# A two-block transformer layer stack on one core: the opening is reordered, TensorE makes three of the eight modulation products, GpSimd none, and VectorE builds the rotation tables after the first activations

## The chip, the cores and the metric

The kernel runs on one core of one Trainium2 chip. The core has five engines with instruction queues of their own: TensorE (PE in the rows), VectorE (DVE), ScalarE (ACT), GpSimd (POOL) and SyncE (SP), which here only issues DMAs. They meet at semaphores alone. The metric is the device time of one execution in microseconds; before the change three timed runs took 1609.88, 1611.33 and 1612.16 us, median 1611.33.

## The reference, cut to what matters

All arithmetic is float32. One sequence of 256 tokens with width 1024 passes a first block (modulated norm, recurrent branch, dilated attention) and a second one (two layers of feed-forward, mixing and embedding parts). The change touches only how the first block begins:

```python
inv_freq = ROPE_THETA ** (-jnp.arange(0, ROT_DIM, 2) / ROT_DIM)
ang = positions[..., None] * inv_freq
cos, sin = jnp.cos(ang), jnp.sin(ang)
c_act = jax.nn.silu(c)                        # c: [1, 1024]
mod = c_act @ w_mod[l] + b_mod[l]             # w_mod: [1024, 3072]
shift, scale, gate = jnp.split(mod, 3, axis=-1)
h = rms_norm(x, g_norm[l]) * (1.0 + scale) + shift
proj = h @ w_in[l]                            # w_in: [1024, 8192]
x_rnn, z_rnn, q, k, v, z_attn, g_r, g_a = jnp.split(proj, IN_SPLITS, axis=-1)
...
qh = apply_partial_rope(q, cos, sin)
kh = apply_partial_rope(k, cos, sin)
```

`shift` and `scale` must be known before the first activation `h`, and `h` before any product with `w_in`. The tables `cos` and `sin` are needed first when q is rotated.

## The kernel before, in words

All weights come from HBM as 245 units of 1 MB (128 partitions by 2048 floats), in the order of use, through a ring of four buffers `raw` (`RING = 4`). Units 0 to 7 hold the shift and scale columns of `w_mod`, 128 rows of it each ("modulation units" 0 to 7 below); the next units are weights proper, called w0, w1, w2, w3 (together the projection to q) and so on. SyncE issues every transfer in one fixed order, and each waits until the buffer's previous content has been used.

A weight unit is split into two parts before TensorE uses it: ScalarE rounds it (`whi`, line 367, `hi`), and the remainder `wlo = raw - whi` is made by VectorE for three units of four (line 1047, `lo`) and by GpSimd for the fourth (line 920). TensorE then makes three products for each piece (lines 1741 to 1743): 12 matmuls of 128x512 for one unit and one half of the tokens. The work of block one goes in slots: 8 slots are a group of four units, first for tokens 0 to 127 (t = 0), then for tokens 128 to 255 (t = 1). The order on each engine is written out by hand; nothing reorders it.

The opening before the change:

- VectorE zeroes `mod_part`, then makes the angles and reduces them to the range of the sine in a chain of small instructions (lines 1149 to 1186), then normalizes the two halves of the rows (line 1189, `xn`).
- The modulation is a product of one row with a 1024x2048 matrix. Unit r times the r-th column of `c_act` gives a 128x2048 product. VectorE adds up six of them (lines 1197 and 1202, `mod_part`), GpSimd makes those of units 0 and 3 (line 959, `MOD_POOL = (0, 3)`, `mod_pool`). TensorE sums each of the three tiles over its partitions: 16 matmuls with one column of ones (line 1864, into `aux`). VectorE adds the three sums and the bias (lines 1207 to 1213, `mod`, `scale_g`).
- TensorE transposes the normalized rows (line 1794, `turn`), VectorE applies scale and shift (line 1221, `full`), ScalarE rounds (line 441, `feed_hi`), VectorE makes the remainder (line 1233, `feed_lo`). With two signals `first_fed` for t = 0 and two for t = 1 TensorE may start the products.
- VectorE then makes a few small vectors of the recurrent gate (lines 1239 to 1268) and waits for the sums of q. ScalarE copies them (line 448), VectorE rotates (lines 1137 to 1142, `rotate`), and TensorE transposes the rotated half at the last slot of the group (slot 7, `block1_turns`), ahead of the last unit of t = 1.

ScalarE applies the sine to the two tables early (lines 431 and 432), before it rounds the first weight unit.

Of the kernel before, what the change touches and what calls it, by code (L numbers as in the profile page):

```python
# [91 lines left out]
MOD_POOL = (0, 3)  # L92
# [10 lines left out]
def build(nc, io):  # L103
    with ExitStack() as ctx:
# [8 lines left out]
        def sb(name, shape, dtype=F32):  # L113
# [69 lines left out]
        mod_pool = [placed("mod_pool0", [P, 2 * D], F32, base[0]),  # L183
                    placed("mod_pool1", [P, 2 * D], F32, base[0] - 4 * HEADS * SEQ)]
# [80 lines left out]
        setup_loaded = sem("setup_loaded")  # L265
        x_loaded = sem("x_loaded")
# [11 lines left out]
        mod_pooled = sem("mod_pooled")  # L278
        mods_ready = sem("mods_ready")
        mod_summed = sem("mod_summed")  # L280
# [53 lines left out]
        def mod_count(r):  # L334

            return sum((k in MOD_POOL) == (r in MOD_POOL) for k in range(r + 1))

        def wait_mod(engine, r):
            engine.wait_ge(mod_pooled if r in MOD_POOL else mod_used, mod_count(r))

# [12 lines left out]
        def _(act):  # L353
# [67 lines left out]
            act.wait_ge(setup_loaded, 16 * 3)  # L421
# [4 lines left out]
            act.wait_ge(lam_abs, 1)  # L426
            act.activation(tiny[:, 2, :], tiny[:, 1, :], ACT.Exp, scale=-1.0).then_inc(lam_exp, 1)
            act.wait_ge(lam_abs, 2)
            act.activation(lb[:, :], tiny[:, 9, 0:A_HEADS], ACT.Sigmoid).then_inc(lb_ready, 1)
            act.wait_ge(angles_ready, 1)  # L430
            act.activation(sin_t[:, :, :], sin_t[:, :, :], ACT.Sin).then_inc(tables_ready, 1)
            act.activation(cos_t[:, :, :], cos_t[:, :, :], ACT.Sin).then_inc(tables_ready, 1)
            hi(RING - 1)

            for t in range(TOK):
                if t:
                    hi()
                for i in range(2):
                    b = next_turn()
                    act.wait_ge(moved[b], (n["tb"] - 1) // 2 + 1)  # L440
                    act.activation(feed_hi[:, 4 * i:4 * i + 4, lanes(t)], full[:, 4 * i:4 * i + 4, lanes(t)],
                                   ACT.Copy).then_inc(fed_hi, 1)

# [445 lines left out]
        def _(pool):  # L889
# [66 lines left out]
            pool.wait_ge(c_ready, 1)  # L956
# [67 lines left out]
        def _(dve):  # L1024
# [120 lines left out]
            mark(dve.memset(mod_part[:, :], 0.0))  # L1145
            dve.wait_ge(setup_loaded, 16 * 3)
# [8 lines left out]

            mark(dve.tensor_copy(pos_f[:, :], pos_i[:, :]))
# [30 lines left out]
            for t in range(TOK):  # L1187
                r = next_rstd()
                dve.tensor_scalar(xn[:, t, :], h[:, t, :], r, None, ALU.mult).then_inc(staged_dve, 1)  # L1189

            dve.wait_ge(c_ready, 1)
            for r in range(N_MOD1):
                if r in MOD_POOL:
                    continue
                dve.wait_ge(loaded[r % RING], 16 * (r // RING + 1))
                if r < N_MOD1 - 1:
                    dve.scalar_tensor_tensor(mod_part[:, :], raw[:, r % RING, :], c_act[:, r:r + 1], mod_part[:, :],
                                             ALU.mult, ALU.add).then_inc(mod_used, 1)
                    dve.wait_ge(mod_used, mod_count(r))
                else:  # L1200
                    for part, signal in ((slice(0, D), mods_ready), (slice(D, 2 * D), mod_used)):
                        dve.scalar_tensor_tensor(mod_part[:, part], raw[:, r % RING, part], c_act[:, r:r + 1],
                                                 mod_part[:, part], ALU.mult, ALU.add).then_inc(signal, 1)
            lo(2)

            dve.wait_ge(mod_summed, 1)
            mark(dve.tensor_tensor(mod[:, :], aux[:, 0, 0:2 * KC], cols[:, COL["b_mod"]:COL["b_mod"] + 2 * KC], ALU.add))
            settle()
            for i in range(len(MOD_POOL)):
                at = 2 * KC * (i + 1)  # L1210
                mark(dve.tensor_tensor(mod[:, :], aux[:, 0, at:at + 2 * KC], mod[:, :], ALU.add))
                settle()
            mark(dve.scalar_tensor_tensor(scale_g[:, :], mod[:, KC:2 * KC], 1.0,
                                          cols[:, COL["g_norm"]:COL["g_norm"] + KC], ALU.add, ALU.mult))
            settle()
# [1043 lines left out]
```

## Time and profile before

| | us |
|---|---|
| median of three timed runs | 1611.33 |
| span of the profiled execution | 1609.2 |
| TensorE busy in the span | 1477.0 |
| first product with a weight unit begins | 52.88 |
| transposes of the first rotated half begin | 73.14 |

The profiled execution is known by its span, from the first to the last instruction; its own device time is not listed apart, so 1609.2 us stands for it. The median of the timed runs is 2.1 us above. Times in rows are from the start of the span. A timeline row merges neighbours of one kind: start, time from the first start to the last end, engine, line, tiles, count, and in brackets how long the engine had been idle and what ended that. One matmul with f32 operands appears as two records in the rows of `aux` and `turn`.

### The profile page before, as it was taken

Reading aid. Unit: us, or ns where it says so; the run is one execution under the profiler, and the core shown is the slowest. Engines: PE = TensorE matmul, PEld = TensorE weight load, DVE = VectorE, ACT = ScalarE, POOL = GpSimd, SP = SyncE. Lnnn points to the kernel's source line nnn. Section 1 sums busy time; section 2 is a strip of 40 time slices with the busy share of each in tenths; the row PEclk is TensorE's granted clock in tenths of the full one; section 3 lists DMA queues with packets and bytes.
Section 4 is the critical chain, followed back from the end, with each engine's and each line's share of the span. In section 5 each row is a group of like instructions: output and inputs, shape, how many; then the busy total and the mean of one; then the engine's idle time right before and its main releaser. Section 6 shows DMA issues by size and latency. Waiting matters only on the chain.

```text
span 1609.2 us, 17128 instructions
## 1 busy us (share of the span) xinstructions
PE 1477.0 (92%) x6606; PEld 1212.3 (75%) x6606; DVE 852.5 (53%) x757; ACT 706.2 (44%) x692; POOL 377.8 (23%) x153
## 2 busy tenths in 40 slices
PE   3999889898999988889999989999999979999896
PEld 3788677676888877667887867878888848888785
DVE  8734775866334457446434474452673343654344
ACT  2545747334344436134444344443443443444332
POOL 3122212213122222003112131222322332322112
PEclk9999999999999999579999999999999979999998
DMA  6745234645455453106544455554643522654441
GB/s 270 292 157 210 105 105 156 236 157 201 162 200 185 163 224 142 46 1 216 184 163 167 179 204 188 209 192 147 234 177 141 206 105 105 229 184 163 169 163 40
DMA packets 40508, 272.51 MB, mean 169 GB/s; under 512 B 4865, under 2 KB 5889, under 8 KB 8834
## 3 DMA queue, kind: packets, MB, share of 16 engines
q1 hardware_dynamic: 36992, 261.65, 44.5%
q10 hardware_dynamic: 3458, 10.04, 1.8%
q8 instruction: 43, 0.70, 0.2%
q14 instruction: 15, 0.12, 0.0%
HBM read 270.62 MB, written 1.05 MB: 169 GB/s over the span
## 4 chain that ended last, share of the span: by engine, by line
PE 73%; DVE 15%; ACT 5%; POOL 3%; issue 3%; DMA 2%; DVEq 0%; SPq 0%; ACTq 0%; POOLq 0%
PE acc L1741 22%; PE acc L1743 22%; PE acc L1742 22%; DVE wlo L1047 5%; PE turn L1794 3%; ACT whi L367 2%; POOL wlo L920 2%; DMA raw<-in_units 1%; DVE h L1117 1%; DVE xn L1101 1%; DVE gate_part L1435 1%; DVE feed_lo L1085 1%; DVE red L1178 0%; DMA gpost<-in_norm_g 0%; PE turn L1895 0%
## 5 line engine op out<-in xcount | busy, mean ns | idle before, releaser
L1047 DVE TENSOR_TENSOR wlo<-raw,whi 128x2048 fp32r<-128x2048 f32 x175 | 463.6, 2664 | 346.5 <-ACT whi L367 346.5
L1741 PE MATMUL acc<-whi,feed_hi 128*128 128x512 f32 (+1 forms) x1504 | 605.8, 403 | 38.9 <-DVE wlo L1047 15.9
L1743 PE MATMUL acc<-whi,feed_lo 128*128 128x512 f32 (+1 forms) x1504 | 593.3, 394 | 0.0
L1742 PE MATMUL acc<-wlo,feed_hi 128*128 128x512 f32 (+1 forms) x1504 | 593.2, 394 | 0.0
L367 ACT ACTIVATE whi<-raw 128x2048 fp32r<-128x2048 f32 x233 | 445.3, 1916 | 326.6 <-PE acc L1743 298.2
L1741 PEld LDWEIGHTS acc<-whi,feed_hi 128*128 128x128 f32 x1504 | 288.6, 192 | 103.2 <-DVE wlo L1047 16.2
L1743 PEld LDWEIGHTS acc<-whi,feed_lo 128*128 128x128 f32 x1504 | 288.0, 191 | 61.9
L1742 PEld LDWEIGHTS acc<-wlo,feed_hi 128*128 128x128 f32 x1504 | 288.9, 192 | 57.3 <-issue 0.2
L928 POOL TENSOR_TENSOR wlo<-raw,whi 128x2048 fp32r<-128x2048 f32 x29 | 133.9, 4618 | 519.9 <-ACT whi L367 519.9
L920 POOL TENSOR_TENSOR wlo<-raw,whi 128x2048 fp32r<-128x2048 f32 x29 | 141.1, 4867 | 393.1 <-ACT whi L367 393.1
L1741 PE MATMUL acc<-whi,hid_hi 128*128 128x512 f32 x352 | 137.8, 392 | 0.0
L1743 PE MATMUL acc<-whi,hid_lo 128*128 128x512 f32 x352 | 137.1, 389 | 0.0
L1742 PE MATMUL acc<-wlo,hid_hi 128*128 128x512 f32 x352 | 137.0, 389 | 0.0
L1464 DVE TENSOR_TENSOR hid_lo<-turn,hid_hi 128x512 f32 (+2 forms) x48 | 30.8, 641 | 88.4 <-ACT hid_hi L595 88.4
L1741 PEld LDWEIGHTS acc<-whi,hid_hi 128*128 128x128 f32 x352 | 66.2, 188 | 13.5
L1743 PEld LDWEIGHTS acc<-whi,hid_lo 128*128 128x128 f32 x352 | 66.1, 188 | 13.7
L1742 PEld LDWEIGHTS acc<-wlo,hid_hi 128*128 128x128 f32 x352 | 66.1, 188 | 13.5
L1794 PE MATMUL turn<-ident,xn 128*128 128x128 f32 x250 | 37.6, 293 | 36.8 <-DVE xn L1189 20.3
L595 ACT ACTIVATE hid_hi<-turn 128x512 f32 (+2 forms) x48 | 26.3, 548 | 99.2 <-PE turn L1794 99.2
L1794 PEld LDWEIGHTS turn<-ident,xn 128*128 128x128 f32 x250 | 31.2, 151 | 43.8 <-issue 23.7
L1455 DVE SCALAR_TENSOR_TENSOR hid<-acc,pre_rs,sgl 128x512 f32<-128x512 f32 (+1 forms) x48 | 33.7, 703 | 48.9 <-ACT sgl L588 43.4
L409 ACT ACTIVATE feed_hi<-turn 128x512 fp32r<-128x512 f32 x52 | 28.9, 592 | 69.8 <-PE turn L1794 69.7
(302 smaller groups left out, 1011.4 us busy)
## 6 DMA issues: line engine op xcount, KB each, us to landing
raw<-in_units SPq DMA_DIRECT2D x245, 1024.0 KB, 4.9
gpost<-in_norm_g ACTq DMA_DIRECT2D x8, 512.0 KB, 4.4
gpre<-in_norm_g ACTq DMA_DIRECT2D x6, 512.0 KB, 6.4
h<-in_x SPq DMA_DIRECT2D x1, 1024.0 KB, 5.9
w_ax<-in_w_ax SPq DMA_DIRECT2D x1, 1024.0 KB, 9.2
bgate<-in_b_gate SPq DMA_DIRECT2D x1, 1024.0 KB, 11.4
out<-h SPq DMA_DIRECT2D x2, 512.0 KB, 2.6
decay<-in_decay ACTq DMA_DIRECT2D x1, 768.0 KB, 4.1
```

The lines of the kernel that those rows point to most:

```text
L367: act.activation(whi[:, u % RING, :], raw[:, u % RING, :], ACT.Copy).then_inc(hi_ready, 1)
L409: act.activation(dst[:, 4 * i:4 * i + 4, lanes(t)], turn[:, b, :].rearrange("p (c s) -> p c s", c=4), ACT.Copy).then_inc(fed_hi, 1)
L595: act.activation(dst, turn[:, b, 0:P * count].rearrange("p (c s) -> p c s", c=count), ACT.Copy).then_inc(fed_hi, 1)
L920: pool.tensor_tensor(wlo[:, RING - 1, :], raw[:, RING - 1, :], whi[:, RING - 1, :].bitcast(F32), ALU.subtract).then_inc(pool_lo, 1)
L928: pool.tensor_tensor(wlo[:, RING - 1, :], raw[:, RING - 1, :], whi[:, RING - 1, :].bitcast(F32), ALU.subtract).then_inc(pool_lo, 1)
L1047: dve.tensor_tensor(wlo[:, u % RING, :], raw[:, u % RING, :], whi[:, u % RING, :].bitcast(F32), ALU.subtract).then_inc(lo_ready, 1)
L1455: dve.scalar_tensor_tensor(hid[:, t, 0:tiles, :], up, pre_rs[:, t:t + 1], sgl[:, t, 0:tiles, :], ALU.mult, ALU.mult)\
L1464: dve.tensor_tensor(hid_lo[:, at, lanes(t)], turn[:, b, 0:P * count].rearrange("p (c s) -> p c s", c=count), hid_hi[:, at, lanes(t)].bitca ...
L1741: pe.matmul(out, xh, wh, start=first, stop=False)
L1742: pe.matmul(out, xh, wl, start=False, stop=False)
L1743: return pe.matmul(out, xl, wh, start=False, stop=last)
L1794: last = pe.transpose(turn[:, b, P * i:P * i + P], part, ident[:, :])
```

## The change

`MOD_POOL = (0, 3)` becomes `MOD_PE = (1, 3, 7)`. TensorE takes units 1, 3 and 7 straight from `raw`: 16 matmuls each, with the unit's 128x128 pieces as weights and the unit's column of `c_act` as the one moving column. VectorE multiplies unit 0 (which also replaces the zeroing) and adds units 2, 4, 5 and 6; TensorE sums that one tile with the ones. GpSimd has no product. Four sums of 16 columns are added in one reduction. `pos_cols` and `invf` are issued by ScalarE. SyncE issues w0 ahead of modulation unit 7. VectorE makes one `lo` before the scales and two (not one) after t = 0. The angles and tables, with their inputs to the gate vectors, come after the activations of t = 1; ScalarE's exponential, sigmoid and the two sines follow its `feed_hi`.

```diff
-MOD_POOL = (0, 3)
+MOD_PE = (1, 3, 7)
...
         # scalar
-            act.wait_ge(setup_loaded, 16 * 3)
+            act.dma_start(pos_i[:, :], io["pos_cols"]).then_inc(angles_loaded, 16)
+            act.dma_start(invf[:, :], io["invf"].partition_broadcast(P)).then_inc(angles_loaded, 16)
+            act.wait_ge(setup_loaded, 16)
             act.activation(c_act[:, :], cols[:, COL["c"]:COL["c"] + KC], ACT.Silu).then_inc(c_ready, 1)
             act.wait_ge(x_loaded, 16 * 2)
             for t in range(TOK):
                 square_sum(h[:, t, :], xn[:, t, :])
-            act.wait_ge(lam_abs, 1)
...
-            act.wait_ge(angles_ready, 1)
-            act.activation(sin_t[:, :, :], sin_t[:, :, :], ACT.Sin).then_inc(tables_ready, 1)
-            act.activation(cos_t[:, :, :], cos_t[:, :, :], ACT.Sin).then_inc(tables_ready, 1)
             hi(RING - 1)
...
+            act.wait_ge(lam_abs, 1)
...
+            act.wait_ge(angles_ready, 1)
+            act.activation(sin_t[:, :, :], sin_t[:, :, :], ACT.Sin).then_inc(tables_ready, 1)
+            act.activation(cos_t[:, :, :], cos_t[:, :, :], ACT.Sin).then_inc(tables_ready, 1)
...
         # sync
-            sp.dma_start(pos_i[:, :], io["pos_cols"]).then_inc(setup_loaded, 16)
-            sp.dma_start(invf[:, :], io["invf"].partition_broadcast(P)).then_inc(setup_loaded, 16)
...
             for r in range(N_MOD1):
                 if r >= RING:
                     wait_mod(sp, r - RING)
+                if r == N_MOD1 - 1:
+
+                    wait_mod(sp, N_MOD1 - RING)
+                    sp.dma_start(raw[:, 0, :], io["units"][N_MOD1]).then_inc(loaded[0], 16)
                 sp.dma_start(raw[:, r % RING, :], io["units"][r]).then_inc(loaded[r % RING], 16)
-            for j in range(RING):
+            for j in range(1, RING):
...
         # gpsimd
-            for r, product in zip(MOD_POOL, mod_pool):
-                pool.wait_ge(loaded[r % RING], 16 * (r // RING + 1))
-                pool.tensor_scalar(product[:, :], raw[:, r % RING, :], c_act[:, r:r + 1], None, ALU.mult)\
-                    .then_inc(mod_pooled, 1)
...
         # vector
+            mod_product(0)
+            for t in range(TOK):
+                r = next_rstd()
+                dve.tensor_scalar(xn[:, t, :], h[:, t, :], r, None, ALU.mult).then_inc(staged_dve, 1)
+
+            for r in range(1, N_MOD1):
+                if r not in MOD_PE:
+                    mod_product(r)
+            lo()
+
+            dve.wait_ge(mod_direct, len(MOD_PE))
+            parts = len(MOD_PE) + 1
+            mark(dve.reduce_sum(mod[:, :], aux[:, 0, 0:2 * KC * parts].rearrange("p (i f) -> p f i", i=parts), AX_X))
+            settle()
...
+                lo(2 if t == 0 else 1)
 
             lam = cols[:, COL["lam"]:COL["lam"] + KC]
...
         # tensor
+            pe.wait_ge(c_ready, 1)
             pe.wait_ge(x_loaded, 16 * 2)
+            mod_direct_unit(0, MOD_PE[0])
             feed_rows(xn[:, 0, :], staged_dve, "dve")
+            mod_direct_unit(1, MOD_PE[1])
             pe.wait_ge(pads_ready, 1)
...
+            pe.wait_ge(mod_used, mod_count(N_MOD1 - 2))
+            mod_columns(len(MOD_PE), mod_part[:, :], ones[:, 0:1])
+            mod_direct_unit(2, MOD_PE[2])
             feed_rows(xn[:, 1, :], staged_dve, "dve")
```

TensorE's queue at the start, before the change: `aux` takes the column sums, `turn` the transposes, `x7` and `x15` are repeats, and in brackets stand the semaphores waited for.

```order
L1794 MATMUL turn<-ident,xn 128x128 [waits staged_dve,x_loaded]
L1794 MATMUL turn<-ident,xn 128x128 x7
L1864 MATMUL aux<-ones,mod_pool_103 128x1 [waits mod_pooled,pads_ready]
L1864 MATMUL aux<-ones,mod_pool_103 128x1 x15
L1864 MATMUL aux<-ones,mod_pool_104 128x1 [waits mod_pooled]
L1864 MATMUL aux<-ones,mod_pool_104 128x1 x15
L1864 MATMUL aux<-ones,mod_part 128x1 [waits mods_ready]
```

And the same place after the change:

```order
L1853 MATMUL aux<-c_act,raw 128x1 [waits loaded1,x_loaded,c_ready]
L1853 MATMUL aux<-c_act,raw 128x1 x15
L1791 MATMUL turn<-ident,xn 128x128 [waits staged_dve]
L1791 MATMUL turn<-ident,xn 128x128 x7
L1853 MATMUL aux<-c_act,raw 128x1 [waits loaded3]
L1853 MATMUL aux<-c_act,raw 128x1 x15
L1853 MATMUL aux<-ones,mod_part 128x1 [waits mod_used,pads_ready]
L1853 MATMUL aux<-ones,mod_part 128x1 x15
L1853 MATMUL aux<-c_act,raw 128x1 [waits loaded3]
```

Three sets of 16 column sums, which came after the transposes, have become four; two stand ahead of the sum of `mod_part`, one of them ahead of the first transposes, and one (unit 7) behind it.

VectorE's queue from the remainders of t = 0 on, before the change (`full` and `feed_lo` are the activations, `tiny` the gate vectors):

```order
L1233 TENSOR_TENSOR feed_lo<-full,feed_hi 128x4x128 [waits fed_hi] x2
L1047 TENSOR_TENSOR wlo<-raw,whi 128x2048 [waits hi_ready]
L1221 TENSOR_SCALAR full<-turn,scale_g,mod 128x128 [waits turned0]
...
L1233 TENSOR_TENSOR feed_lo<-full,feed_hi 128x4x128 [waits fed_hi] x2
L1239 TENSOR_SCALAR tiny<-tiny 128x8 [waits lam_exp]
...
L1137 TENSOR_TENSOR rope_a<-xn,cos_t 128x256 [waits tables_ready,acc_free0]
```

And after the change:

```order
L1190 TENSOR_TENSOR feed_lo<-full,feed_hi 128x4x128 [waits fed_hi] x2
L1043 TENSOR_TENSOR wlo<-raw,whi 128x2048 [waits hi_ready] x2
L1178 TENSOR_SCALAR full<-turn,scale_g,mod 128x128 [waits turned0]
...
L1190 TENSOR_TENSOR feed_lo<-full,feed_hi 128x4x128 [waits fed_hi] x2
L1195 TENSOR_SCALAR tiny<-cols 128x8
...
L1203 CAST pos_f<-pos_i 128x4 [waits angles_loaded]
...
L1233 MEMSET tiny 128x8 [waits dve_step]
L1236 TENSOR_SCALAR tiny<-tiny 128x8 [waits lam_exp]
...
L1133 TENSOR_TENSOR rope_a<-xn,cos_t 128x256 [waits tables_ready,acc_free0]
```

One more `wlo` stands between the two halves of the activations, and the whole making of the tables (`pos_f` to the second `MEMSET`) between the activations of t = 1 and the first rotation.

## Rows read from the trace of the kernel before

**Rows 1.** The page of the profiled execution: its head.
```profile
span 1609.2 us, 17128 instructions
```

**Rows 2.** Timeline of the opening: start us, us, engine, line; merged rows.
```profile
2.12 0.43 SPq L846 DMA_DIRECT2D h<-in_x  x1
...
6.29 0.17 DVE L1149 TENSOR_SCALAR tiny<-cols 128x8 f32<-128x8 f32 x1 [3.29 <-DMA invf<-in_invf]
...
7.68 0.34 DVE L1172 TENSOR_SCALAR trn<-ang 128x352 f32<-128x352 f32 x1
...
11.05 0.35 DVE L1172 TENSOR_SCALAR trn<-ang 128x352 f32<-128x352 f32 x1
...
20.27 1.94 PE L1794 MATMUL turn<-ident,xn 128*128 128x128 f32 x8 [20.27 <-DVE xn L1189]
...
22.01 13.65 PE L1864 MATMUL aux<-ones,mod_pool 128*128 128x1 f32 x64
25.90 7.11 DVE L1197 SCALAR_TENSOR_TENSOR mod_part<-raw,c_act,mod_part 128x2048 f32<-128x2048 f32 x3
...
39.95 6.98 PE L1864 MATMUL aux<-ones,mod_part 128*128 128x1 f32 x32 [4.29 <-DVE mod_part L1202]
...
47.66 0.17 DVE L1207 TENSOR_TENSOR mod<-aux,cols 128x16 f32<-128x16 f32 x1
...
48.48 2.90 DVE L1221 TENSOR_SCALAR full<-turn,scale_g,mod 128x128 f32<-128x128 f32 x8
```

**Rows 3.** Timeline from the first activations to the rotation; same columns.
```profile
52.01 1.89 ACT L367 ACTIVATE whi<-raw 128x2048 fp32r<-128x2048 f32 x1
...
52.75 2.28 DVE L1047 TENSOR_TENSOR wlo<-raw,whi 128x2048 fp32r<-128x2048 f32 x1
52.88 0.80 PE L1741 MATMUL acc<-whi,feed_hi 128*128 128x512 f32 x1 [0.33 <-DVE feed_lo L1233]
...
53.99 5.52 POOL L920 TENSOR_TENSOR wlo<-raw,whi 128x2048 fp32r<-128x2048 f32 x1 [28.56 <-ACT whi L367]
...
57.76 2.90 DVE L1233 TENSOR_TENSOR feed_lo<-full,feed_hi 128x512 fp32r<-128x512 f32 x2
...
60.58 0.16 DVE L1239 TENSOR_SCALAR tiny<-tiny 128x8 f32<-128x8 f32 x1
...
66.23 0.43 DVE L1137 TENSOR_TENSOR rope_a<-xn,cos_t 128x256 f32<-128x256 f32 x1 [1.42 <-ACT xn L448]
...
67.10 0.42 DVE L1142 TENSOR_TENSOR xn<-rope_a,rope_b 128x256 f32<-128x256 f32 x1
```

**Rows 4.** Timeline of TensorE: the transposes of the first rotated half.
```profile
73.14 1.03 PE L1794 MATMUL turn<-ident,xn 128*128 128x128 f32 x8
```

**Rows 5.** Line 851's second and third transfers: issues, and issue to landing (us).
```profile
L851 SPq DMA_DIRECT2D raw<-in_units x2: 627/668/710, 3.6 to 4.2; - x2
...
DMA to landing us min/median/max: 11.2/12.1/13.0
```

**Rows 6.** Line 851's sixth transfer, on an empty queue; same columns.
```profile
L851 SPq DMA_DIRECT2D raw<-in_units x1: 327/327/327, 28.3 to 28.3; - x1
...
DMA to landing us min/median/max: 4.8/4.8/4.8
```

**Rows 7.** Timeline later: a GpSimd remainder started just before a VectorE one.
```profile
338.50 4.96 POOL L920 TENSOR_TENSOR wlo<-raw,whi 128x2048 fp32r<-128x2048 f32 x1 [16.99 <-ACT whi L367]
338.94 6.67 DVE L1047 TENSOR_TENSOR wlo<-raw,whi 128x2048 fp32r<-128x2048 f32 x1
...
345.66 0.80 PE L1741 MATMUL acc<-whi,feed_hi 128*128 128x512 f32 x1 [3.23 <-DVE wlo L1047]
...
348.80 0.40 PE L1742 MATMUL acc<-wlo,feed_hi 128*128 128x512 f32 x1
...
349.72 0.39 PE L1743 MATMUL acc<-whi,feed_lo 128*128 128x512 f32 x1
```

**Rows 8.** TensorE after that wait: window, busy times (PE first), granted clock.
```profile
346.00:348.00 2.00, 2.00 (x6) 1.52 (x6) 0.00 (x0) 0.00 (x0) 0.00 (x0) 0.50 0.54 139
```

More of the change, by code:

```diff
@@ L265, in build @@
         setup_loaded = sem("setup_loaded")
+        angles_loaded = sem("angles_loaded")
         x_loaded = sem("x_loaded")
@@ L334, in mod_count @@
         def mod_count(r):
-            return sum((k in MOD_POOL) == (r in MOD_POOL) for k in range(r + 1))
+            return sum((k in MOD_PE) == (r in MOD_PE) for k in range(r + 1))
         def wait_mod(engine, r):
-            engine.wait_ge(mod_pooled if r in MOD_POOL else mod_used, mod_count(r))
+            engine.wait_ge(mod_direct if r in MOD_PE else mod_used, mod_count(r))
         def chunks(ap, n=4):
@@ new lines, in _ @@
+            settle()
+            mark(dve.tensor_tensor(mod[:, :], mod[:, :], cols[:, COL["b_mod"]:COL["b_mod"] + 2 * KC], ALU.add))
+            settle()
+            mark(dve.scalar_tensor_tensor(scale_g[:, :], mod[:, KC:2 * KC], 1.0,
+                                          cols[:, COL["g_norm"]:COL["g_norm"] + KC], ALU.add, ALU.mult))
+            settle()
+            for t in range(TOK):
+                for i in range(2):
+                    b = next_turn()
+                    for c in range(4):
+                        f = 4 * i + c
+                        ins = dve.tensor_scalar(full[:, f, lanes(t)], turn[:, b, P * c:P * c + P],
+                                                scale_g[:, f:f + 1], mod[:, f:f + 1], ALU.mult, ALU.add)
+                        if c < 3:
+                            mark(ins)
+                            if c == 2:
+                                settle()
+                        else:
+                            ins.then_inc(moved[b], 1)
+                for i in range(2):
+                    n["fed"] += 1
+                    dve.wait_ge(fed_hi, n["fed"])
+                    part = (slice(None), slice(4 * i, 4 * i + 4), lanes(t))
+                    dve.tensor_tensor(feed_lo[part], full[part], feed_hi[part].bitcast(F32), ALU.subtract)\
+                        .then_inc(first_fed, 1)
+                lo(2 if t == 0 else 1)
@@ L1186, in _ @@
             dve.memset(tiny[:, 4, :], 0.0).then_inc(angles_ready, 1)
[L1187 to L1214, printed above, removed]
@@ L1849, in group_deep, with mod_columns, mod_direct_unit @@
                         hooks[2]()
+            def mod_columns(i, part, by):
+                for f in range(2 * KC):
+                    at = 2 * KC * i + f
+                    last = pe.matmul(aux[:, 0, at:at + 1], part[:, P * f:P * f + P], by, start=True, stop=True)
+                return last
+            def mod_direct_unit(i, r):
+                pe.wait_ge(loaded[r % RING], 16 * (r // RING + 1))
+                mod_columns(i, raw[:, r % RING, :], c_act[:, r:r + 1]).then_inc(mod_direct, 1)
+            pe.wait_ge(c_ready, 1)
             pe.wait_ge(x_loaded, 16 * 2)
+            mod_direct_unit(0, MOD_PE[0])
             feed_rows(xn[:, 0, :], staged_dve, "dve")
+            mod_direct_unit(1, MOD_PE[1])
             pe.wait_ge(pads_ready, 1)
-            for i, part in enumerate(mod_pool + [mod_part]):
-                if part is not mod_part:
-                    pe.wait_ge(mod_pooled, i + 1)
-                for f in range(2 * KC):
-                    if part is mod_part and f == 0:
-                        pe.wait_ge(mods_ready, 1)
-                    if part is mod_part and f == KC:
-                        pe.wait_ge(mod_used, mod_count(N_MOD1 - 1))
-                    at = 2 * KC * i + f
-                    last = pe.matmul(aux[:, 0, at:at + 1], part[:, P * f:P * f + P], ones[:, 0:1],
-                                     start=True, stop=True)
-            last.then_inc(mod_summed, 1)
+            pe.wait_ge(mod_used, mod_count(N_MOD1 - 2))
+            mod_columns(len(MOD_PE), mod_part[:, :], ones[:, 0:1])
+            mod_direct_unit(2, MOD_PE[2])
             feed_rows(xn[:, 1, :], staged_dve, "dve")
```

48 lines of the change are left out of this document (16 added, 32 removed).

## The prediction

> **What bounds the kernel now.** I read the head of the page first (the profiled execution, 1609.2 us [rows 1], against a median of 1611.33), then the timeline of the opening, the one stretch that the edit touches. Behind it every engine is paced by TensorE, so a shift of TensorE at the end of the opening should stay to the end of the kernel. Four points matter.
>
> First, the column sums of the modulation end at 39.95 + 6.98 = 46.93 us; VectorE is then still in a remainder and takes the sums up at 47.66; the scales are ready at 48.48 [rows 2]. I call that moment S.
>
> Second, from S on the chain is fixed: 8 scalings and two remainders last until VectorE's next remainder at 52.75 (S + 4.3), the first product of w0 starts at 52.88 (S + 4.4) [rows 3].
>
> Third, the reader is to see slack in front of the first rotation. VectorE waits 1.42 us for the sums of q at 66.23 and has rotated at 67.10 + 0.42 = 67.5 [rows 3]; TensorE comes to the transposes at 73.14 and has no wait there (the row shows no bracket) [rows 4]. So 5.6 us of VectorE's time are free between S and S + 24.7.
>
> Fourth, the column sums are slow: 16 of them take 7.0 us, alone or in a pair (13.65 for two sets) [rows 2].
>
> **The change part by part.**
>
> *Start of TensorE's products.* SyncE no longer issues the two small transfers ahead of x, which was issued at 2.12 and took 0.43 to issue [rows 2]; all later issues come about 0.9 us earlier. Modulation unit 1 landed at 3.6 + 11.2 = 14.8, unit 2 at 4.2 + 13.0 = 17.2 [rows 5]. I take 13.9 for unit 1 (bounds: 14.8 if bandwidth alone decides; 12.9 if leaving out the small transfers saves as much again). TensorE: unit 1 from 13.9 to 20.9 (7.0); 8 transposes 22.01 - 20.27 = 1.7, to 22.6; unit 3, long there, to 29.5.
>
> *VectorE's products.* They follow the landings: unit 2, there at 17.2 - 0.9 = 16.3, is added by 18.7, and VectorE waits. The buffer of unit 5 is that of unit 1, free at 20.9. On an empty queue 1 MB lands 4.8 us after its issue [rows 6], so unit 5 is there at 25.7 and unit 6, 2.5 later, at 28.2. A product costs 7.11 / 3 = 2.37 [rows 2], so VectorE's sum is whole at 30.6. TensorE: sum of `mod_part` 30.6 to 37.6, unit 7 (issued at 29.9, landed by 37) 37.6 to 44.6. VectorE then needs three small instructions where four took 48.48 - 47.66 = 0.8 [rows 2]: 0.7 with the wake-up. S becomes 45.3, a gain of 3.2 us. Bounds: 44.2 to 46.5 from unit 1's landing and the landing times. GpSimd's products and the zeroing go at no gain of their own: they lay beside other work.
>
> *The second remainder after t = 0.* VectorE makes w1 and w2 there; w1 was made before S in the old order. It starts w2 at S + 4.3 + 2.3, less a tenth of overlap, = 51.8 [rows 3]. Meanwhile w3 can be issued only when TensorE has finished unit 7: 44.6 + 4.8 = 49.4, ScalarE's rounding takes 1.9 [rows 3], and GpSimd starts its remainder of w3 at 51.4, some 0.4 us ahead of VectorE. Later in the trace there is the same pair: GpSimd starts at 338.50, VectorE 0.44 later, and VectorE ends at 345.61, after GpSimd's 343.46, having taken 6.67 for 2.28 of work [rows 7, 3]. In the other order GpSimd waits: its 5.52 from 53.99 hold 1.0 of VectorE's remainder and 4.5 of its own [rows 3]. So VectorE finishes w2 at 51.4 + 4.5 + 2.2 = 58.1 and not at 54.0. TensorE wants w2 at about 56.5 (S + 4.4, then two units) and loses 1.6, which the next wait swallows. Bounds of this term: 0 if VectorE is first and nothing meets, 4.1 as here.
>
> The Trainium skill has this as a rule (SBUF — State Buffer, "SBUF: two separate sides"): the port pair that VectorE and GpSimd share is an exclusive lock, and "the other fully blocks". By that rule, the pair at 338.50 agrees. The rule speaks against this change: it takes GpSimd out of the products, but brings its w3 next to VectorE's w2, and by it the sum is the one below; without it the forecast would be the third case.
>
> *The tables.* They stand now behind the activations of t = 1. Those need 4.3 from 58.1: 62.4. Angles and the small ones ahead of them 7.68 - 6.29 = 1.4, the sine table 11.05 - 7.68 = 3.4 [rows 2], the cosine table one instruction more, 3.7, and the last step 0.1: 8.6, undisturbed, since GpSimd is done at 55.9. That gives 71.0. The gate vectors and the rotation are 67.5 - 60.6 - 1.4 (the wait) = 5.5 [rows 3]: 76.5. Behind the tables on VectorE queue the remainders of w4 and w5; on ScalarE, which waits for the angles before its sines, the copy of q's sums and the roundings of w4 to w6. These end before TensorE wants them, since TensorE itself is held at the transposes.
>
> *What TensorE sees.* It could transpose at 45.3 + 24.7 = 70.0, or 71.6 with the wait for w2, and gets the rotated half at 76.5: 3.4 later than the 73.14 of before, after 4.9 us without work. After a wait of 3.23 its clock was at 0.50 granted, the lower of its levels, 1.2 GHz [rows 7, 8]: seven matmuls took 348.80 - 345.66 = 3.1, where four more took 0.9 [rows 7]. That is 0.45 against 0.23, 1.5 us lost. I add it whole: 3.4 + 1.5 = 4.9 us over the 1609.2 of the profiled execution, and with the median as the base 1611.33 + 4.9 = 1616.2.
>
> **The rivals.**
>
> *VectorE wins the race for the shared port* (24 in 100). The landing of w3 need only be 0.4 longer. Then w2 is ready at 54.0, GpSimd runs 54.0 to 58.5, and the two remainders of t = 1 wait for it, as in the 2.90 from 57.76 [rows 3]; they end at 59.8. The tables end at 68.4, the rotation at 73.9: 0.8 late, TensorE idle for 3.9, clock lost again: +2.3, 1613.6.
>
> *Nothing collides* (14 in 100). w2 at 54.0, t = 1 ready at 58.3, rotation at 72.4: 0.7 early, a wait of 2.4, no loss of clock: 1610.6. For it speaks only that the port does not hold every pair up; against it the two rows above.
>
> *TensorE warms up in the column sums* (7 in 100), so that it is faster than before. Unit 1 to unit 7 is nearly 31 us of work with short gaps. At the higher level a set would take 3.5 us; unit 5 could be issued at 17.4, and S would come some 8 us sooner, at 37.5. The rotation, 31.2 behind S, is at 68.7: 4.4 sooner than 73.14, 1.5 lost again: about 1608.4. Against it: the 13.65 us of column sums in a row did not get faster, the set after them still took 6.98 [rows 2].
>
> *The tables cost more than their own time* (8 in 100): unit 1 lands at 14.8, or ScalarE's sine blocks the rounding of w4 so that another unit is late and the pair w6 and w7 meets in the wrong order, another 4.1. Price up to 1620.
>
> The edit could fail to do what it says only if the products stayed on VectorE; the listing of the queues excludes that.
>
> **How the numbers follow.** The forecast has 47 in 100, with its own range 1615 to 1618. What a measurement can tell from no change is 0.2%, 3.2 us: slower is above 1614.6, faster below 1608.1. Slower: 42 of the forecast's 47, 4 of the first rival's 24, all 8 of the last: 54. Faster: half of the warm case and 3 for what I have missed: 6. Same: 40. The range for 8 in 10 leaves out the warm case and the far end of the last: 1610.4 to 1618.5.
>
> **What would show it.** Right: 16 column sums still take 7.0; TensorE's opening sums end near 44.6; the first product of w0 begins near 49.7; GpSimd's first remainder starts just ahead of VectorE's third and that one takes over 6 us; the longest new wait of TensorE is that of the transposes of the rotated half, 4 to 5 us, on line 1138; granted clock 0.5 behind it. Wrong: column sums of 3.5, tables done before the sums of q, or a VectorE remainder of w2 at 2.3 us.

## The result, and the profile after

The changed kernel takes 1617.04 us (median of five runs, 1615.59 to 1617.48) against 1610.72 us (also a median of five) for the kernel before. The ratio is 1.0046, 95% interval [1.0027, 1.0064]; ratios here are estimates with an interval and not the quotients of the two medians (that would be 1.0039). In a later comparison, with twelve runs of the changed kernel, the ratio was 1.0040 [1.0022, 1.0057]: slower, by 6.4 to 7.4 us. The forecast was 1616.2 us. The profiled execution has a span of 1613.7 us, 4.5 more than that of before [rows 1].

The timeline of the opening after the change; columns as in [rows 2]:

```profile
13.73 6.96 PE L1853 MATMUL aux<-c_act,raw 128*128 128x1 f32 x32 [13.73 <-DMA raw<-in_units]
...
22.28 6.83 PE L1853 MATMUL aux<-c_act,raw 128*128 128x1 f32 x32
25.58 4.83 DVE L1149 SCALAR_TENSOR_TENSOR mod_part<-raw,c_act,mod_part 128x2048 f32<-128x2048 f32 x2 [2.20 <-DMA raw<-in_units]
...
30.55 6.96 PE L1853 MATMUL aux<-ones,mod_part 128*128 128x1 f32 x32 [1.44 <-DVE mod_part L1149]
...
37.74 6.99 PE L1853 MATMUL aux<-c_act,raw 128*128 128x1 f32 x32 [0.23 <-DMA raw<-in_units]
44.77 0.22 DVE L1166 TENSOR_REDUCE mod<-aux 128x16 f32<-128x64 f32 x1 [6.39 <-PE aux L1853]
...
45.43 2.90 DVE L1178 TENSOR_SCALAR full<-turn,scale_g,mod 128x128 f32<-128x128 f32 x8
```

Four sets of column sums, of 6.8 to 7.0 us each, follow each other on TensorE with short gaps and the first transposes between them, and end at 44.73, where three ended at 46.93 before. S, the moment at which the scales are ready, is 45.43 against 48.48 [rows 2]: 3.05 earlier. Up to here the change is ahead.

From the first activations to the rotation, all engines; same columns:

```profile
49.63 1.91 ACT L364 ACTIVATE whi<-raw 128x2048 fp32r<-128x2048 f32 x1 [0.58 <-DMA raw<-in_units]
49.70 8.88 DVE L1043 TENSOR_TENSOR wlo<-raw,whi 128x2048 fp32r<-128x2048 f32 x2
...
51.62 4.81 POOL L921 TENSOR_TENSOR wlo<-raw,whi 128x2048 fp32r<-128x2048 f32 x1 [39.07 <-ACT whi L364]
...
58.63 0.50 PE L1738 MATMUL acc<-whi,feed_hi 128*128 128x512 f32 x1 [1.68 <-DVE wlo L1043]
...
67.13 0.34 DVE L1231 TENSOR_SCALAR sin_t<-red 128x352 f32<-128x352 f32 x1
...
70.88 0.34 DVE L1231 TENSOR_SCALAR cos_t<-red 128x352 f32<-128x352 f32 x1
```

Two remainders of VectorE, 2.28 us each on their own [rows 3], take 8.88: the second one, of w2, is made beside GpSimd's of w3 and ends 2.1 us after it. In the kernel before, the same moment of the program had VectorE first (52.75) and GpSimd second (53.99) [rows 3], and w2 was ready at 55.0. It is ready at 58.58 now although everything ahead of it came 3 us sooner. The tables begin behind the activations of t = 1, at 62.76, and end at 71.3.

TensorE's waits in that stretch and what follows the second of them; same columns:

```profile
76.75 1.97 PE L1791 MATMUL turn<-ident,xn 128*128 128x128 f32 x8 [4.23 <-DVE xn L1138]
78.37 0.77 PE L1738 MATMUL acc<-whi,feed_hi 128*128 128x512 f32 x1
78.94 0.63 PE L1739 MATMUL acc<-wlo,feed_hi 128*128 128x512 f32 x1
79.37 0.63 PE L1740 MATMUL acc<-whi,feed_lo 128*128 128x512 f32 x1
```

Windows over the same place: window, its length, busy time of PE, PEld, DVE, ACT, POOL with counts, then the granted clock, the DMA share and GB/s:

```profile
74.00:76.00 2.00, 0.00 (x0) 0.00 (x0) 1.85 (x11) 2.00 (x2) 0.00 (x0) 1.00 0.00 0
76.00:78.00 2.00, 1.25 (x6) 1.25 (x7) 1.97 (x4) 2.00 (x2) 0.00 (x0) 0.68 0.00 0
78.00:80.00 2.00, 2.00 (x8) 1.71 (x7) 2.00 (x2) 1.19 (x2) 0.00 (x0) 0.50 0.00 0
80.00:82.00 2.00, 2.00 (x9) 1.63 (x9) 1.70 (x2) 0.00 (x0) 0.00 (x0) 0.96 0.93 283
```

TensorE is out of work from 72.52 to 76.75, while VectorE is busy without a gap. The transposes of the first rotated half take 1.97 where they took 1.03 [rows 4], and the matmuls behind them follow each other at 0.43 us where 0.23 is usual: granted clock 0.50, the lower of TensorE's two levels, 1.2 GHz. The next transposes start at 90.20 against 84.93 before, the third ones at 102.30 against 97.05. So 3.61 us late at the first, 5.27 and 5.25 late at the second and third. From there to the end of the profiled execution the changed kernel needs 1511.4 us and the kernel before 1512.15, which is nearly the same.

How the waits group, after the change: line waited at and its releaser, us in total, times, longest.

```profile
PE acc L1738 <- DVE wlo L1043: 18.1, 5, 6.6
...
PE turn L1791 <- DVE xn L1138: 4.9, 3, 4.2
```

The first group had 15.9 us in 4 waits before, and TensorE waited for the rotated halves for 0.6 us in all, at most 0.3. The two new waits of the opening are among these: 1.7 us for w2 and 4.2 us for the first rotated half.

### The profile page after: what moved, and what is told of

It is laid out like the page before. It is cut to its first block, busy times and chain, and to the rows that moved or that the text cites. A ratio compares the mean times of both kernels' runs of the same rounds, so it can differ in the third digit from the quotient of the medians.

```text
span 1613.7 us, 17185 instructions
## 1 busy us (share of the span) xinstructions
PE 1488.1 (92%) x6638; PEld 1222.0 (76%) x6638; DVE 839.6 (52%) x753; ACT 706.0 (44%) x692; POOL 367.0 (23%) x151
## 3 DMA queue, kind: packets, MB, share of 16 engines
q1 hardware_dynamic: 36704, 261.56, 44.6%
## 4 chain that ended last, share of the span: by engine, by line
PE 73%; DVE 15%; ACT 5%; issue 3%; POOL 3%; DMA 2%; SPq 0%; DVEq 0%; ACTq 0%; POOLq 0%
PE acc L1738 22%; PE acc L1740 21%; PE acc L1739 21%; DVE wlo L1043 6%; PE turn L1791 4%; ACT whi L364 2%; POOL wlo L921 2%; DMA raw<-in_units 1%; PE aux L1853 1%; DVE h L1113 1%; DVE xn L1097 1%; DVE feed_lo L1081 1%; DVE gate_part L1432 0%; DMA gpost<-in_norm_g 0%; PE turn L1897 0%
## 5 line engine op out<-in xcount | busy, mean ns | idle before, releaser
L1081 DVE TENSOR_TENSOR feed_lo<-turn,feed_hi 128x512 fp32r<-128x512 f32 x52 | 34.1, 686 | 40.0 <-ACT feed_hi L406 39.8
```

Source lines behind the costliest of these rows:

```text
L1081: dve.tensor_tensor(dst[part], turn[:, b, :].rearrange("p (c s) -> p c s", c=4), hi_part[part].bitcast(F32), ALU.subtract).then_inc(moved[ ...
```

## The experiments

Each kernel is the changed one with an edit, except tables_late, which is the kernel before with an edit. Since the part behind the opening differs by several us between executions of one program (below), each is judged first by the start of the first, second and third transposes (at the third ones the matmuls go at their usual pace again), then by its time. A ratio whose interval holds 1 can't be told from the kernel before:

| kernel | S | transposes 1, 2, 3 | third, against before | ratio to before, 95% interval |
|---|---|---|---|---|
| before | 48.48 | 73.14, 84.93, 97.05 | 0 | 1 |
| changed | 45.43 | 76.75, 90.20, 102.30 | +5.3 | 1.0046 [1.0027, 1.0064] |
| after_again | 45.45 | 76.79, 89.94, 102.09 | +5.0 | 1.0040 [1.0022, 1.0057] |
| dve_first | 45.92 | 74.48, 87.67, 99.77 | +2.7 | 1.0021 [1.0005, 1.0037] |
| tables_gap | 46.00 | 74.54, 86.33, 98.45 | +1.4 | 1.0011 [0.9997, 1.0025] |
| filler | 45.71 | 78.32, 90.13, 102.25 | +5.2 | 1.0013 [0.9997, 1.0029] |
| w1_early | 46.09 | 72.16, 84.02, 96.14 | -0.9 | 1.0001 [0.9985, 1.0016] |
| both | 45.72 | 71.16, 82.96, 95.07 | -2.0 | 0.9997 [0.9977, 1.0018] |
| products_only | 46.32 | 71.40, 83.20, 95.31 | -1.7 | 0.9986 [0.9971, 1.0002] |
| tables_late | 44.71 | 70.79, 82.64, 94.76 | -2.3 | 0.9983 [0.9961, 1.0005] |
| best | 42.29 | 67.15, 78.95, 91.06 | -6.0 | 0.9964 [0.9947, 0.9981] |
| best2 | 42.02 | 67.09, 78.87, 90.98 | -6.1 | 0.9969 [0.9957, 0.9980] |

### tables_gap: the tables in VectorE's idle time

VectorE is idle from the end of unit 6's product to the first remainder, some 5.5 us, and again until the column sums end. The tables go there, ahead of `lo()`, and on ScalarE the exp, the sigmoid and the sines behind the rounding of w0:

```diff
                 if r not in MOD_PE:
                     mod_product(r)
+            # lam, angles, both reductions (the code moved up from behind the activations)
             lo()
-            (same code, behind the activations of t = 1)
```

> The changed kernel with one part undone: VectorE makes angles and tables in its idle time behind the product of unit 6 (30.4 to 39 us), ScalarE its exponential, sigmoid and sines behind the rounding of w0. Theory (late tables hold the first rotation): TensorE reaches the transposes of the rotated half at 72.4 us and waits for nothing there; 4.2 us of wait and 1.1 us of low clock behind it go, the wait of 1.7 us for w2 stays; span 1608.4 against 1613.7 of the changed kernel, about 0.8 us under the kernel before. Rival (the loss comes from the collision of the remainders of w2 and w3 alone): the span stays within 1 us of 1613.

Measured: TensorE has no wait at the transposes, as expected, and the third ones come at 98.45 instead of 102.30. So moving the tables gives back 3.9 of the 5.25 us, clock loss included; the rival is out. But the transposes start at 74.54 and not at 72.4, and the span is 1610.4 and not 1608.4: TensorE itself was late. Its timeline there, then windows of the same run:

```profile
59.21 0.50 PE L1739 MATMUL acc<-whi,feed_hi 128*128 128x512 f32 x1 [1.95 <-DVE wlo L1044]
74.54 1.04 PE L1792 MATMUL turn<-ident,xn 128*128 128x128 f32 x8
```

```profile
59.00:61.00 2.00, 1.79 (x5) 1.45 (x6) 1.96 (x7) 0.35 (x1) 0.00 (x0) 0.66 1.01 426
61.00:63.00 2.00, 2.00 (x6) 1.54 (x6) 1.80 (x5) 0.92 (x2) 0.00 (x0) 0.50 0.95 377
```

S was 0.57 later (unit 1 landed at 14.24 instead of 13.73; in filler, where nothing ahead of S is changed, S is 0.28 later). The wait for w2 was still there with 1.95 us, and it cost the clock: nine steps from 59.21 to 62.87, 3.66 us where 2.04 is usual, so 1.6 us. So a second cost of the change lies in w2, which the wait for the tables had hidden.

### w1_early: the old order of the remainders

```diff
-            lo()
+            lo(2)
...
-                lo(2 if t == 0 else 1)
+                lo(1)
```

> The changed kernel with VectorE's remainder of w1 moved in front of the scales (idle there from 38.4 to 44.8 us), so that w2 is the first one behind t = 0; tables stay late. Theory (GpSimd's w3, started 0.35 us before VectorE's w2, blocks it for 4.3 us, and everything behind on VectorE is late by that): w2 takes 2.3 us from 49.7, the rotation is done near 71.8 instead of 76.7, TensorE waits about 1.2 us there without losing clock; span near 1607.7. Rival (the tables alone set the time of the rotation): the wait stays at 3 us or more and the span above 1611.

VectorE and GpSimd, from the first activations on, and TensorE's first and third transposes:

```profile
50.34 2.28 DVE L1043 TENSOR_TENSOR wlo<-raw,whi 128x2048 fp32r<-128x2048 f32 x1
...
52.21 4.90 POOL L921 TENSOR_TENSOR wlo<-raw,whi 128x2048 fp32r<-128x2048 f32 x1 [39.13 <-ACT whi L364]
...
52.55 2.89 DVE L1178 TENSOR_SCALAR full<-turn,scale_g,mod 128x128 f32<-128x128 f32 x8
...
55.36 2.90 DVE L1190 TENSOR_TENSOR feed_lo<-full,feed_hi 128x512 fp32r<-128x512 f32 x2
...
72.16 1.10 PE L1791 MATMUL turn<-ident,xn 128*128 128x128 f32 x8 [1.00 <-DVE xn L1138]
...
96.14 1.03 PE L1791 MATMUL turn<-ident,xn 128*128 128x128 f32 x8
```

With w1's remainder back ahead of the scales, w2's starts at 50.34, 1.9 us ahead of GpSimd's w3, and takes its usual 2.28. VectorE goes on beside GpSimd with the scalings, which read PSUM, at their usual 2.89. Only the two remainders of t = 1, which read two operands in SBUF, are held up: 2.90 for a pair that takes 1.53 in the changed kernel. TensorE's wait for w2 is gone, the one at the rotation is 1.00 and costs no clock. The third transposes are at 96.14, so this one place in the order made 6.2 us, more than the whole loss: 4.6 by the earlier rotation and 1.6 by the clock. The ratio says the same: 1.0001 [0.9985, 1.0016], below both intervals of the changed kernel. The tables still stand behind the activations here, and the rival (the tables alone) is out.

### dve_first: the collision turned round, nothing else

```diff
+                if u == RING - 1:
+                    pool.wait_ge(lo_ready, RING - 1)
```

> The changed kernel with one wait added: GpSimd starts its first remainder (w3) only when VectorE has finished w2. Theory (whoever starts first holds the port): w2 takes 2.3 us and is done at 54.3, GpSimd runs to 58.8, the two remainders of t = 1 wait for it and end near 60.0, the rotation near 74.1, TensorE waits 3.5 us and still loses clock; span near 1611.1, so holding GpSimd back by 2.7 us gains 2.6 us. Rival (VectorE's 6.6 us of w2 have another cause than GpSimd): w2 still takes over 5 us, span 1613.7 or more.

```profile
50.19 4.49 DVE L1045 TENSOR_TENSOR wlo<-raw,whi 128x2048 fp32r<-128x2048 f32 x2
...
54.82 4.61 POOL L923 TENSOR_TENSOR wlo<-raw,whi 128x2048 fp32r<-128x2048 f32 x1 [42.21 <-DVE wlo L1045]
...
74.48 1.97 PE L1793 MATMUL turn<-ident,xn 128*128 128x128 f32 x8 [3.42 <-DVE xn L1140]
```

The same two remainders in 4.49 instead of 8.88: the 4.4 us came from GpSimd's w3 running beside w2, and not from the data or its landing; the rival is out. TensorE's wait for w2 is gone, the one at the transposes is 3.42 and does cost the clock (1.97 for the transposes). Of the 4.4 us 2.3 show at the first transposes and 2.5 at the third: GpSimd's late w3 holds up the two remainders of t = 1 (3.18, where 1.53 pass between 61.31 and 62.84 in the changed kernel), and S was 0.5 later in this run.

### filler: the clock alone

18 matmuls of 128x512 whose results nobody reads stand ahead of the transposes, so that TensorE works where it waited.

```diff
+                        if g == 0:
+                            for _ in range(18):
+                                pe.matmul(aux[:, 1, :], feed_hi[:, 0, lanes(1)], whi[:, RING - 1, 0:BANK],
+                                          start=True, stop=True)
```

> The changed kernel with 18 extra matmuls of 128x512 on TensorE (into an unused bank, results not used) ahead of the transposes of the first rotated half, so that TensorE works through the 4.2 us in which it waited. Theory (the wait costs twice, the second time by the clock granted behind it): the transposes start at 76.7 as before, the matmuls behind them follow at 0.23 us from the first one, the granted clock stays at 1.00, and the next transposes come 1.1 to 1.5 us earlier than at 90.20; span near 1612.4. Rival (the slow matmuls behind the wait have nothing to do with the idle time): no change, 1613.7.

TensorE, and the clock in windows:

```profile
58.94 0.79 PE L1738 MATMUL acc<-whi,feed_hi 128*128 128x512 f32 x1 [2.15 <-DVE wlo L1043]
74.24 4.25 PE L1943 MATMUL aux<-whi,feed_hi 128*128 128x512 f32 x18
78.32 1.03 PE L1791 MATMUL turn<-ident,xn 128*128 128x128 f32 x8
90.13 1.04 PE L1791 MATMUL turn<-ident,xn 128*128 128x128 f32 x8
```

```profile
76.00:78.00 2.00, 2.00 (x10) 1.65 (x10) 1.97 (x5) 2.00 (x2) 0.00 (x0) 1.00 0.00 0
78.00:80.00 2.00, 2.00 (x15) 1.74 (x14) 2.00 (x2) 1.50 (x2) 0.00 (x0) 1.00 0.00 0
```

The transposes start 1.57 us later than in the changed kernel, for TensorE had lost its clock at w2 and came at 74.24, and the 18 matmuls take 4.1 us. So the next transposes are no earlier than in the changed kernel (90.13 against 90.20), other than expected. But they come 11.81 us behind the first ones instead of 13.45, with the granted clock at 1.00. So the drop of the clock behind the 4.2 us wait costs 1.64 us (prediction: 1.5), and the rival is out. The time (1.0013) is below what the third transposes let expect (+5.2 us would be 1.0032). In the profile 3.8 us are missing, and 2.5 of them lie between the last transposes of `xn` (1383.9; before 1380.0) and the last ones of `hid` (1516.4; before 1515.0). Why that stretch differs is open.

### both: tables in the idle time and the old order

The two edits of tables_gap and w1_early together. (In the recorded texts of both, products_only and best, w1 and w2 are exchanged: it is w1's remainder that goes ahead of the scales, and w2's that stays behind t = 0.)

> The changed kernel with two places mended at once: the tables in VectorE's idle time after unit 6 (as in tables_gap), and w2's remainder before the scales, w1's behind t=0 (as in w1_early). Theory (the 3.3 us of loss against the kernel before are two orders on VectorE: tables behind the activations, w1's remainder ahead of w2's in the race with GpSimd): S at about 46.0 (VectorE's work ahead of it ends some 0.5 later than in the changed kernel), first product about 50.5, no wait for w2 beyond GpSimd's own, the transposes of the first rotated half at about 71.2 without a wait, 1.9 earlier than in the kernel before (73.14), and the time some 2 us below the kernel before. Rival (the scales' gain is lost in any case, for w1's remainder and the rotation stand in its place): transposes at 73 to 74.5, time the kernel before's or above.

The transposes at 71.16 without a wait, the third at 95.07, 2.0 before the kernel before: as expected to 0.1 us. The time shows it less clearly: 0.9997 [0.9977, 1.0018] holds both no change and the 2 us (0.9988).

### tables_late and products_only: each half of the change alone

tables_late is the kernel before with lines 1148 to 1186 behind the activations and ScalarE's exponential, sigmoid and two sines with them:

```diff
             mark(dve.memset(mod_part[:, :], 0.0))
             dve.wait_ge(setup_loaded, 16 * 3)
-            # lam, angles, both reductions
...
                 lo()
+            # lam, angles, both reductions
             dve.wait_ge(lam_exp, 1)
```

> The kernel before, with nothing of the products changed; only the tables (and ScalarE's exp, sigmoid and two sines) go behind the first activations, as in the changed kernel. It is the second half of the change alone. Theory: VectorE starts on unit 1 some 1 to 2 us earlier but waits for the landings and shares its port with GpSimd's products all the same, so that S comes at 46 to 48; GpSimd's w3 and VectorE's w2 collide as before; the tables (8.6 us) then stand in front of the rotation, the transposes at 76 to 79 and some 3 us of time added: the late tables cost more than the early products give. Rival: the products end 4 us earlier, as the tables' whole length goes from ahead of them, and the transposes come at 71 to 73, time the same or 2 us lower.

products_only is the changed kernel with the tables (and their two transfers, on SyncE) ahead of the products, and the remainders in the old order:

```diff
             sp.dma_start(cols[:, :], io["cols"]).then_inc(setup_loaded, 16)
+            sp.dma_start(pos_i[:, :], io["pos_cols"]).then_inc(angles_loaded, 16)
+            sp.dma_start(invf[:, :], io["invf"].partition_broadcast(P)).then_inc(angles_loaded, 16)
...
+            # lam, angles, both reductions
             mod_product(0)
...
-            lo()
+            lo(2)
```

> The first half of the change alone: TensorE makes units 1, 3 and 7, VectorE the other five, GpSimd none; the tables (and their two transfers) stand where they do in the kernel before, and w2's remainder comes ahead of w1's, as there. Theory: S is set by TensorE's four column sums, which the tables don't touch (in the changed kernel and in both, the fourth of them ends at 44.7), so S at 45.4 to 46.5, the transposes of the first rotated half at 71 to 72, time 1 to 2 us below the kernel before. With tables_late (S at 44.7, GpSimd's products left as they were) it would say that either half alone brings the scales 2 to 4 us forward and that they don't add. Rival: with 9 us of tables first, VectorE's products end late as in the kernel before, S at 47.5 or later and the time that of the kernel before.

tables_late, the products and what ends them; then products_only:

```profile
19.35 12.83 DVE L1159 SCALAR_TENSOR_TENSOR mod_part<-raw,c_act,mod_part 128x2048 f32<-128x2048 f32 x4
...
39.19 2.29 DVE L1047 TENSOR_TENSOR wlo<-raw,whi 128x2048 fp32r<-128x2048 f32 x1 [1.87 <-ACT whi L367]
41.68 2.29 DVE L1047 TENSOR_TENSOR wlo<-raw,whi 128x2048 fp32r<-128x2048 f32 x1 [0.20 <-ACT whi L367]
43.89 0.17 DVE L1169 TENSOR_TENSOR mod<-aux,cols 128x16 f32<-128x16 f32 x1
```

```profile
17.00 2.35 DVE L1149 SCALAR_TENSOR_TENSOR mod_part<-raw,c_act,mod_part 128x2048 f32<-128x2048 f32 x1 [0.23 <-DMA raw<-in_units]
...
43.03 2.29 DVE L1043 TENSOR_TENSOR wlo<-raw,whi 128x2048 fp32r<-128x2048 f32 x1 [4.06 <-ACT whi L364]
45.65 0.23 DVE L1206 TENSOR_REDUCE mod<-aux 128x16 f32<-128x64 f32 x1 [0.32 <-PE aux L1853]
```

Moving the tables alone brings S from 48.48 to 44.71, more than the whole change (45.43), though GpSimd's two products stretch VectorE's first four to 12.83 (four times 2.35 without them). My theory for tables_late fails: I had S at 46 to 48 and the transposes at 76 to 79. The rival (71 to 73) comes close: the transposes are at 70.79. The late tables alone cost next to nothing: the table code begins at 56.78, for w2 (from 48.97) started ahead of GpSimd's w3 (50.22), and the rotation is ready nearly as TensorE arrives (a wait of 0.34). Moving the products alone brings S to 46.32, 2.2 earlier than before, and the transposes to 71.40, both inside the ranges of its text. So each half brings the scales 2.2 to 3.8 us forward, and they don't add.

### best and best2: what the runs point to

In the changed kernel S comes 0.7 us behind the last of four sets of column sums. best has only unit 4 on TensorE (`MOD_PE = (4,)`), seven on VectorE, the units in plain order, the tables first, the old order of the remainders. best2 also sums the last product in two halves.

```diff
-MOD_PE = (1, 3, 7)
+MOD_PE = (4,)
...
-            pe.wait_ge(mod_used, mod_count(N_MOD1 - 2))
+            pe.wait_ge(mod_used, mod_count(N_MOD1 - 1))
             mod_columns(len(MOD_PE), mod_part[:, :], ones[:, 0:1])
-            mod_direct_unit(2, MOD_PE[2])
```

> Only unit 4 goes to TensorE, VectorE makes the other seven, GpSimd none; the tables stand first on VectorE as in the kernel before, w2's remainder ahead of w1's. Theory (what held the scales in the changed kernel are TensorE's slow column sums, four of 7.0 us; with two, the landings and VectorE's products bound it): column sums end near 38.7, S at about 39.5, the first product near 43.9, the transposes of the first rotated half near 64.6, the time some 8 us below the kernel before. Rival (the weight units and their remainders, not the scales, bound what follows): the transposes at 69 or later, time at most 4 us below.

> The kernel best with the last unit's product in two halves, each summed as soon as it is made (as in the kernel before). In best unit 7 lands at 32.1, its product takes 2.35 and TensorE starts its sums at 34.66. Theory (the scales wait for the last landing): sums start at 33.5, S at 41.2, 1.1 earlier than in best (42.3), the transposes of the first rotated half at 66.1 against 67.2, ratio to the kernel before 0.0007 lower than best's. Rival (the remainders of the weights bound what follows): S comes earlier, the transposes don't.

best, VectorE and TensorE:

```profile
32.16 2.35 DVE L1145 SCALAR_TENSOR_TENSOR mod_part<-raw,c_act,mod_part 128x2048 f32<-128x2048 f32 x1 [0.85 <-DMA raw<-in_units]
...
34.66 6.96 PE L1849 MATMUL aux<-ones,mod_part 128*128 128x1 f32 x32 [5.13 <-DVE mod_part L1145]
...
41.66 0.19 DVE L1202 TENSOR_REDUCE mod<-aux 128x16 f32<-128x32 f32 x1 [0.32 <-PE aux L1849]
...
67.15 1.03 PE L1787 MATMUL turn<-ident,xn 128*128 128x128 f32 x8
```

best is faster than both kernels: 1602.61 us against 1609.65, ratio 0.9964 [0.9947, 0.9981]. S is 42.29, not 39.5, and the transposes are at 67.15, not 64.6: VectorE waits for units 6 and 7 to land (0.36 and 0.85 us), and I had the last product end 3 us too early. The transposes come 6.0 us sooner than before (8 were expected, at most 4 by the rival), and the 5.8 us of the ratio agree. Which of the parts gives how much was not tested; against products_only, which has the same order of tables and remainders, best differs in the number of sets of column sums (two, not four), the order of the transfers and VectorE's share. best2's sums start 0.94 sooner (33.72), but S gains only 0.27: VectorE is in w1's remainder until 41.39. The transposes gain 0.06, and 0.9969 [0.9957, 0.9980] can't be told from best. So its rival fits: S comes earlier, and the transposes hardly do.

### after_again: the same kernel once more

> The changed kernel once more, beside the others on one chip: span 1613.7 to 1615.6, transposes of the first rotated half at 76.7 or, in an execution where the 1.7 us wait for w2 costs TensorE its clock, some 1.5 later; ratio to the kernel before 1.003 to 1.005. Rival (the first comparison's 0.46% was partly the chip): within 0.2%.

The ratio is 1.0040, the third transposes are 0.2 from those of the first profile. TensorE, behind the wait for w2:

```profile
58.67 0.50 PE L1738 MATMUL acc<-whi,feed_hi 128*128 128x512 f32 x1 [1.96 <-DVE wlo L1043]
59.01 0.58 PE L1739 MATMUL acc<-wlo,feed_hi 128*128 128x512 f32 x1
59.39 0.63 PE L1740 MATMUL acc<-whi,feed_lo 128*128 128x512 f32 x1
```

This time the wait for w2 cost the clock too. It made no difference to the first transposes: TensorE came to the transposes at 74.2 instead of 72.5 and waited 2.6 instead of 4.2 us. The span is 2.7 us longer than in the first profile all the same. Both are level at 171 us (ScalarE's first write of `yat`, 171.4 and 171.2) and 2.8 apart at 654 (VectorE's first copy into `att_a`, 653.7 and 656.5), with one wait for ScalarE at 2.2 us instead of 0.6 between them. That is how much two executions of one kernel can differ behind the opening.

## Why the prediction was right, point by point

- *Start of TensorE's products, S.* Unit 1 at 13.73 (13.9), VectorE's sum whole at 30.4 (30.6), column sums end 44.73 (44.6), S 45.43 (45.3). A set still takes 6.96, so the rival of a TensorE that warms up is out.
- *The remainder of w2.* GpSimd starts at 51.62 (51.4), w2 is done at 58.58 (58.1), TensorE loses 1.68 (1.6). dve_first shows that the cause is GpSimd's w3. The prediction gave 24 in 100 to the race going the other way; GpSimd was ahead by some 0.3 to 0.4 us in all four runs with this order. dve_first builds that other case: priced at +2.3 us, it comes to +2.7 at the third transposes.
- *The tables.* 8.5 us from 62.76 (8.6 from 62.4), rotation done at 76.70 (76.5).
- *What TensorE sees.* It reached the transposes at 72.52, not 71.6, and waited 4.23 instead of 4.9. Of the 0.9 us, 0.2 are S and the longer wait for w2, and 0.3 lie in the matmuls behind the first product, which stayed longer at a pace of 0.43; the rest lies around the two waits. Start 76.75: 3.61 late (3.4). The clock cost 1.64 (1.5; filler). At the third transposes 5.25, predicted 4.9.
- *That the wait for w2 is swallowed.* In the changed kernel yes, with or without a loss of clock (after_again). But the working takes the step at 1.6 us, and it is worth more as soon as the tables are out of the way: 1.95 and some 1.6 of clock in tables_gap. The costs overlap and don't add: curing the tables alone gives back 3.9, the order of the remainders alone 6.2, both 7.2. The rival in which nothing collides has a wait of 2.4 us and no loss of clock; the waits of 1.95, 1.96 and 2.15 us all lost it, so that price was too low.
- *Where the reading was short.* The sum needs both the collision and the tables' new place, and the prediction does not ask what each is worth alone. tables_late and w1_early show that this place costs 0.3 and 1.0 us of waiting once w2 does not collide. The root is one remainder moved, `lo(2)` turned into `lo()` before the scales: it puts w1 into VectorE's busiest stretch, w2 into GpSimd's port time, and with that the tables into TensorE's sight. The prediction had all three links, but no term for leaving w1 where it was.
- *A row misread.* The prediction says of GpSimd's products that they lay beside other work. In the kernel before they held VectorE up:

```profile
19.75 5.69 POOL L959 TENSOR_SCALAR mod_pool<-raw,c_act 128x2048 f32<-128x2048 f32 x1 [0.98 <-DMA raw<-in_units]
20.04 5.93 DVE L1189 TENSOR_SCALAR xn<-h,rs 128x1024 f32<-128x1024 f32 x1
```

The same normalization takes 0.74 just ahead of it, and with GpSimd idle (products_only) the two tables take 7.2 us instead of 11.7. This did not enter the sum, in which TensorE's chain sets S. That products_only gains its 2.2 us from it is likely, but not shown.

The profile's 4.5 us and the 6.4 to 7.4 us of the two ratios are apart, but the intervals (from 3.5 and 4.3 us up) hold the 5.25 of the transposes. That the forecast time is within 0.8 us of the measured median is in part luck: 4.9 us were added to a base of 1611.33, and the five runs of the kernel before that stand beside the result have 1610.72, so that the difference of the medians is 6.3.

## What to carry to other kernels

When a change moves work between engines, follow the instruction that it pushes next to another engine's, not only the one that it moves: here 2.3 us of a remainder moved by one place cost 6.2. Before a long step is called late, ask what held up the work ahead of it. And put the parts of such a change to the test one by one: products and tables alone were each some 2 us ahead of the kernel before at the third transposes, both together (w1_early) 0.9 ahead, and with w1's remainder moved as well 5.3 behind.

## What the runs showed of the hardware that was not expected

- VectorE beside GpSimd's `tensor_tensor`: a remainder with two SBUF inputs stands still (6.6 us for 2.28), scalings from PSUM do not (2.89 beside it and 2.90 without). GpSimd won with a lead of 0.3 to 0.4 us in four runs, VectorE with 1.2 to 1.9 us in seven others; what decides in between was not tested. The Trainium skill says of the port pair (SBUF — State Buffer, "SBUF: two separate sides") that whichever of the two starts first holds it for the whole instruction and the other fully blocks, and it counts for VectorE only operations in a two-port mode or with two SBUF inputs. The trace agrees: 6.6 us for the remainder, no change for the scalings.
- A wait of about 2 us may or may not cost TensorE its clock. The one of 1.68 us did not; those of 1.95, 1.96 and 2.15 did (eight or nine steps of mostly 0.43 us, 1.6 to 1.7 us lost each), and so did those of 2.63, 3.42 and 4.23. The granted clock doesn't tell all: it reads 1.00 from 50 to 52 in the changed kernel, while the first matmuls behind the opening follow each other at 0.43 us as well (49.84 to 52.56, six steps; 0.45 each).
- A sum over the partitions by TensorE (128x128 by one column, float32) takes 6.8 to 7.0 us for 16 of them, 32 records of 0.22 us, at a granted clock of 1.00, and in no run less, even at the end of 31 us of nearly unbroken work of that kind.
- The two profiled executions of the changed kernel differ by 2.7 us, all of it behind the opening. Timed ones spread further: 31 of the kernel before beside tables_gap took 1598.90 to 1614.46 us. For a change of 0.3% the start of a row shortly after the change says more than one span.
